# A two-layer decoder in fp32 on one core: the residual comes back in four pieces, and casts, remainders and token sums change places in their engines' orders

## What is computed

```python
def swiglu(h, w_gate_up, w_down):
    gu = h @ w_gate_up
    return (jax.nn.silu(gu[..., :D_FF]) * gu[..., D_FF:]) @ w_down

x = x + jnp.concatenate([main_out, mem_out], axis=-1) @ w_out[l]
return x + swiglu(rms_norm(x, ffn_norm[l]), w_gate_up[l], w_down[l])
```

## Time and profile before

| | |
|---|---|
| median of 3 runs | 3159.64 us |
| the profiled execution | 3156.6 us |
| its span in the trace | 3154.4 us |
| granted TensorE clock, mean over the span | 0.96 of full speed |
| PE busy | 2875.1 us (91% of the span) |
| DVE, ACT, POOL busy | 1487.3, 933.2, 1098.5 us |
| DMA queue | 257 MB, 25.4% of 16 engines |
| phase_ffn, layer 0 | from 1013.6 us to about 1704 us |
| phase_ffn, layer 1 | from 2448.3 us to about 3138 us |

### The profile page before, as it was taken

The page is one execution under the profiler, slowest core; times in us unless marked ns, Lnnn a source line. Parts: engine busy times, 40 slices in busy tenths (PEclk is TensorE's granted clock), DMA queues, the critical chain, the costliest instruction groups (busy, mean ns, idle before and its releaser), DMA issues. The chain is left out here.

```text
span 3154.4 us, 54822 instructions
## 1 busy us (share of the span) xinstructions
PE 2875.1 (91%) x23385; PEld 2311.3 (73%) x23385; DVE 1487.3 (47%) x2032; ACT 933.2 (30%) x1522; POOL 1098.5 (35%) x1050
## 2 busy tenths in 40 slices
PE   7999589888689999998999979969979999998998
PEld 5888367777557788886887767746648788886887
DVE  6233256666343655543223636547742755444222
ACT  3111334332143433332002123135542533332100
POOL 5343033333122444444334223311102344444332
PEclk9999699999799999999999989989989999999999
DMA  5332200000042232235223222233113133225321
GB/s 200 102 109 69 89 17 23 23 30 4 15 135 74 61 107 80 88 93 162 75 80 115 77 74 67 80 120 116 46 34 134 47 108 91 89 81 156 96 76 66
DMA packets 261081, 261.16 MB, mean 83 GB/s; under 512 B 9254, under 2 KB 221340, under 8 KB 259560
## 3 DMA queue, kind: packets, MB, share of 16 engines
q1 hardware_dynamic: 260088, 257.00, 25.4%
q10 hardware_dynamic: 272, 0.63, 0.1%
q0 software_dynamic: 480, 0.03, 0.0%
HBM read 186.80 MB, written 70.83 MB: 82 GB/s over the span
## 5 line engine op out<-in xcount | busy, mean ns | idle before, releaser
L276 POOL TENSOR_TENSOR w_lo_b<-w_raw_b,w_hi_b 128x512 fp32r<-128x512 f32 (+1 forms) x474 | 592.5, 1251 | 404.2 <-ACT w_hi_b L308 386.4
L358 PE MATMUL ps<-b_hi,w_hi_b 128*128 128x512 f32 x1176 | 459.2, 390 | 10.1 <-DVE b_lo L2233 7.3
L358 PE MATMUL ps<-b_lo,w_hi_b 128*128 128x512 f32 x1176 | 458.8, 390 | 0.0
L358 PE MATMUL ps<-b_hi,w_lo_b 128*128 128x512 f32 x1176 | 458.7, 390 | 0.0
L272 POOL CAST w_hi_b<-w_raw_b 128x384 fp32r<-128x384 f32 (+1 forms) x222 | 132.2, 596 | 799.5 <-PE ps L330 586.6
L358 PEld LDWEIGHTS ps<-b_hi,w_hi_b 128*128 128x128 f32 x1176 | 221.5, 188 | 57.8 <-DVE b_lo L2233 8.1
L330 PE MATMUL ps<-b_hi,w_hi_b 128*128 128x512 f32 x768 | 241.6, 396 | 22.2 <-DVE x_res L2308 22.2
L358 PEld LDWEIGHTS ps<-b_hi,w_lo_b 128*128 128x128 f32 x1176 | 221.5, 188 | 46.4
L358 PEld LDWEIGHTS ps<-b_lo,w_hi_b 128*128 128x128 f32 x1176 | 221.5, 188 | 45.8
L330 PE MATMUL ps<-b_lo,w_hi_b 128*128 128x512 f32 x768 | 239.9, 394 | 0.0
L330 PE MATMUL ps<-b_hi,w_lo_b 128*128 128x512 f32 x768 | 239.6, 393 | 0.0
(11 more groups left out here) (334 smaller groups left out, 5619.2 us busy)
## 6 DMA issues: line engine op xcount, KB each, us to landing
w_raw_b<-in_w_gate_up SPq DMA_DIRECT2D x88, 512.0 KB, 4.3
act_dram<-x_res SPq DMA_DIRECT2D x44, 512.0 KB, 6.0
stage<-act_dram SPq DMA_DIRECT2D x44, 512.0 KB, 3.6
w_raw_b<-in_w_down SPq DMA_DIRECT2D x32, 384.0 KB, 3.8
w_raw_a<-in_a_w_in SPq DMA_DIRECT2D x23, 512.0 KB, 4.7
u_dram<-evac_a SPq DMA_DIRECT2D x23, 512.0 KB, 3.0
w_raw_b<-in_w_down SPq DMA_DIRECT2D x32, 320.0 KB, 3.2
x_dram<-x_res SPq DMA_DIRECT2D x2, 4096.0 KB, 14.5
```

The lines of the kernel that those rows point to most:

```text
L276: nc.gpsimd.tensor_tensor(self.wlo[:, r, 0:n, :], source, self.whi[:, r, 0:n, :].bitcast(F32), ALU.subtract).then_inc(self.w_lo, 1)
L358: mm = self.nc.tensor.matmul(self.ps[:, bank, :], w[:, r, k, :], h[:, block, k, :], start=(start and k == 0 and a == 0 and h is self.bh), ...
```

## The change

It does seven things, all in `phase_ffn`:

1. The residual's H2 half comes back in four DMAs of 512 KB in place of two of 1 MB, in the order tiles 4-5, 0-1, 6-7, 2-3. The first stands right behind the store of feature tile 20 on SP, the second behind the load of tile 5, the third behind the store of feature tile 21, the fourth behind the load of tile 7.
2. `FF_ORDER` is 4, 5, 0, 1, 6, 7, 2, 3, and DVE waits for a piece ahead of each second addition of the first group.
3. In the last pair, DVE's remainders of tiles 2, 3 stand behind the addition to up, and those of tiles 4, 5 behind `scale_gate`.
4. The token sums stand in front of step k = 2 of the first projection.
5. On ACT `cast_sum(0)` and `cast_sum(1)` stand ahead of the first copy out of PSUM, and `cast_sum(2)` and the casts of weight blocks 2 to 4 have new places.
6. `silu(0)` stands behind the first copy of pair 1.
7. On DVE `sum_rest(0)` and `sum_rest(1)` stand ahead of `late_sums`.

The diff, cut to its core:

```diff
-FF_ORDER = [4, 5, 6, 7, 0, 1, 2, 3]
+FF_ORDER = [4, 5, 0, 1, 6, 7, 2, 3]
...
@@ SP
+                back = lambda tiles, semaphore: sp.dma_start(X[:, tiles, H2], self.x_dram[:, tiles, H2]).then_inc(semaphore, 16)
+                back(slice(4, 6), x_gate[0])
                 for t in range(2, groups[0][1]):
                     load_tile(t)
-                sp.wait_ge(act_full, FT)
-                sp.dma_start(X[:, HK:KT, H2], self.x_dram[:, HK:KT, H2]).then_inc(x_gate, 16)
+                sp.wait_ge(act_stored[0], 16 * (FT // 2))
+                back(slice(0, 2), x_up[0])
                 store(FT - 1)
-                for f in (FT - 2, FT - 1):
-                    sp.wait_ge(act_stored[f % 2], 16 * (f // 2 + 1))
-                sp.dma_start(X[:, 0:HK, H2], self.x_dram[:, 0:HK, H2]).then_inc(x_up, 16)
+                back(slice(6, 8), x_gate[1])
                 for g in range(G):
                     for i in range(KT):
                         load_upto(d0 + KT * g + i + 4)
                         if g + 1 < G and i < groups[g + 1][1]:
                             load_tile(groups[g + 1][0] + i)
+                        if g == 0 and i == 1:
+                            sp.wait_ge(act_stored[1], 16 * (FT // 2))
+                            back(slice(2, 4), x_up[1])
...
@@ ACT
-                for i in range(3):
+                for i in range(2):
                     self.cast_block(act, first(1) + i)
+                cast_sum(0)
+                cast_sum(1)
                 act.wait_ge(self.block_done, self.done(u0))
-                act.wait_ge(t_formed, 2)
                 copy(gate(0), ps[:, 0:2, :]).then_inc(snapped, 1)
-                for i in range(3, 5):
+                for i in range(2, 4):
                     self.cast_block(act, first(1) + i)
-                for n in range(3):
-                    cast_sum(n)
+                cast_sum(2)
+                self.cast_block(act, first(1) + 4)
...
                 cast_sum(3)
-                silu(0)
                 for f in range(1, FT):
...
                     copy(gate(f)[:, 0, :], ps[:, b, :]).then_inc(snapped, 1)
+                    if f == 1:
+                        silu(0)
...
@@ DVE
                 self.early_sums(dve, u0 + 2)
+                sum_rest(0)
+                sum_rest(1)
                 self.late_sums(dve, u0 + 2)
-                for n in range(3):
-                    sum_rest(n)
+                sum_rest(2)
...
-                    for t in range(4 if last else 0):
+                    for t in range(2 if last else 0):
                         tile_rest(t)
...
-                    for t in range(4, groups[0][1] if last else 4):
+                    for t in range(2, 4 if last else 2):
                         tile_rest(t)
...
                     scale_gate(f)
+                    for t in range(4, groups[0][1] if last else 4):
+                        tile_rest(t)
                     scale_up(f)
...
-                        if n == 0:
-                            dve.wait_ge(x_gate, 16)
-                        if n == HK:
-                            dve.wait_ge(x_up, 16)
+                        if n < KT and i % 2 == 0:
+                            dve.wait_ge((x_gate[0], x_up[0], x_gate[1], x_up[1])[i // 2], 16)
...
@@ PE
-                for t in range(TT):
-                    mm = mmul(ps[:, 6, t:t + 1], acc[:, t * P:(t + 1) * P], self.const("ones"), start=True, stop=True)
-                mm.then_inc(self.sums, 1)
-
...
+                def sum_tokens(k):
+                    if k == 2:
+                        for t in range(TT):
+                            mm = mmul(ps[:, 6, t:t + 1], acc[:, t * P:(t + 1) * P], self.const("ones"), start=True, stop=True)
+                        mm.then_inc(self.sums, 1)
+                    pe.wait_ge(self.h_lo, k + 1)
+
-                self.plain_gemm(pe, u0, base(0), operand, before_k=lambda k: pe.wait_ge(self.h_lo, k + 1))
+                self.plain_gemm(pe, u0, base(0), operand, before_k=sum_tokens)
```

2 lines of the change are left out of this document (1 added, 1 removed).

## The result

The changed kernel takes 3137.4 us (median of 4 runs, 3136.4 to 3140.3). The kernel before, run beside it on the same chip, takes 3158.1 us (median of 4). The ratio is 0.9939, with a 95% interval of 0.9921 to 0.9958: 20.6 us faster, where 22.4 were forecast, and 3137.2 us was the number. The profiled execution took 3140.3 us, its span is 3138.4 us, 16.0 less than before.

What follows compares the result with a forecast made beforehand. PE, busy for 91% of the span, was taken as the bound, with its pauses and the clock drops after them. 5.0 - 1.0 + 16.2 + 2.2 = 22.4 us off 3156.6 gives 3134.2, plus 3.0 makes 3137.2 us; range 3125 to 3148.

Steps and rivals of the forecast that it cites:

- start: Start of the phase through pair 1: one layer in each of two clock cases, gain 5.0 us in all.
- last pair: Last pair: the first piece ahead of tile 3's load delays it 0.5 us each layer, together -1.0.
- pause before strip 2: Before down strip 2: PE's pause falls from 10.96 to 2.9 us, gain 16.2 us over both layers.
- clock behind it: After the pause before strip 2: 1.7 us lost to half clock each layer, 5.6 together before; gain 2.2.
- the good case: Phase start: the clock rises at about 6 us in spite of the token sums; gain 4.5 us a layer.
- the bad case: Phase start: the token sums break the clock's rise, 14.4 us at half clock; gain 0.5 us a layer.
- Now the store goes at 1457.0: SP's queue before strip 2: last store at 1457.0, tile 6's cast starts at 1466.0, PE resumes at 1469.9.
- The bad clock case in both layers: Rival, phase start: the sums break the clock's rise in both layers; gain 18.4 us, 3141 us, chance 0.18.
- the good one in both layers: Rival, phase start: the sums do not matter to the clock in either layer; 26.4 us, 3133 us, chance 0.20.
- The crowding rival: Rival, before strip 2: four 512 KB transfers crowd, tile 6 some 3 us later, 6 us pause; 3143 us, chance 0.08.
- the change doesn't reach the pause: Rival, before strip 2: something unnamed holds tile 6 until the old moment; only 4 us gained, 3155.6 us, chance 0.04.
- a queue starts which makes PE wait in strip 0: Rival, tile loads: the piece ahead starts a queue, loads land after 14 us; slower, 3185 us, chance 0.02.

Runs made afterwards that it cites:

- sums_k1: The changed kernel with the token sums ahead of step k = 1 in place of k = 2; 3139.9 us (1 run).
- pieces_silu: The kernel before with only the four pieces, FF_ORDER, DVE's waits and silu(0) behind pair 1's first copy; 3137.3 us (5 runs), ratio 0.9935.
- piece2_late: The changed kernel with the second piece (tiles 0, 1) issued behind the last store and the third piece; 3139.3 us (1 run).
- sums_front: The changed kernel with the token sums back in front of the first projection; 3136.8 us (4 runs), ratio 0.9933.
- pieces_only: The kernel before with only the four pieces, FF_ORDER and DVE's waits for them; 3144.1 us (4 runs), ratio 0.9951.
- tiles_early_cast3: tiles_early with ACT's cast of tile 3 behind the copy of up in the last pair; 3120.9 us (4 runs), ratio 0.9873.
- tiles_early: The changed kernel with the loads of tiles 6 and 7 ahead of the last store, the second piece behind it; 3129.7 us (4 runs), ratio 0.9905.

## Why the prediction was right, and where it was not

| term, both layers | forecast | measured |
|---|---|---|
| start | 5.0 | 8.5 |
| last pair | -1.0 | -0.6 |
| pause before strip 2 | 16.2 | 13.45 |
| clock behind it | 2.2 | 1.1 |
| sum | 22.4 | 22.35 |

The first part of the table of phases holds the first two terms: 4.00 + 3.84 = 7.84, and with the 0.22 + 0.41 us that the last pair lost, the start gave 8.5.

**The start was mis-sized by 3.5 us, and the failed step is the choice between the two clock cases.** "I see them as equally likely in each layer and take one of each: 5.0 us in all" priced the good case at 4.5 a layer. It came in both layers (4.2 each). In all kernels with the sums two steps in or ahead the rise came at most 6.2 us after the projection's start. Only sums_k1, which puts the sums ahead of that point, brings out the bad case, and there it costs 1.6 us, not 4.0: the stretch at half clock grows by about the sums' own time. The text had the row that decides this. It had worked out 5.1 us to the sums and 6.2 us to the rise, so at most 1.1 us of the sums could stand ahead of it. And it had priced the bad case with 5.7 us more at half clock behind the sums, which no row had shown, and sums_k1 had 3.4 and 3.3. The working by parts was sound otherwise: silu's move alone gives 3.5 and 3.0 us, and the remaining 1 us comes with the casts and remainders (start part 455.7 / 455.6 in pieces_silu, 454.7 / 454.7 with them).

**The pause was mis-sized by 2.75 us, and the failed step is "Now the store goes at 1457.0".** The rest of the chain held: from the store's issue to the cast 8.64 us (forecast 9.0), from the cast to PE 4.05 (3.9). But the store was issued at 1462.33. This execution's phase began 7.75 us later and its start part was 4.00 shorter, so on the old time scale that is 1458.6, 1.6 us late. The reason is the sentence "Feature tile 21 ... comes about 1 us earlier". It came 0.6 us later (1462.31 on the old scale is 1458.6, against 1457.94). I had looked at what stands ahead of tile 21 on DVE, and not at what stands ahead of it on ACT, where silu and the up copy wait behind the cast of tile 5. Tile 5's load landed in 5.6 and 5.5 us. I had taken 3.5 from the earlier trace rows, a median. Two neighbours have come close to it, the load of tile 4 1.1 us ahead (2.8 before) and the second piece 0.4 us behind, and the table at piece2_late shows 0.9 us more with the first alone and 0.9 to 2 with both. The landings of stage's loads in the same stretch after, in the view of its DMAs, are longer as a whole, which doesn't say by what:

```profile
stage<-act_dram SPq DMA_DIRECT2D x10, 512.0 KB, 4.1
```

The median is 4.1 us, and was 3.5. How large the miss came out is in part this trace's own: with the same code the pause is 3.34 to 4.19 us in sums_front and sums_k1, so 0.4 to 1.3 us above the forecast's 2.9 in place of 1.4 and 1.5. The Trainium skill (DMA: Bandwidth & Descriptors, Rules for kernel authors) asks for 1 MiB or more per DMA for the most bandwidth. Taken alone, that speaks against the four pieces. The ratio of pieces_only, 0.9951, says that in this kernel the moment at which a transfer can start was worth more than its rate.

**The clock behind the pause.** 1.1 in place of 2.2 us: 5.5 and 2.9 us at half clock remained where 3.4 were taken for each, and the 5.2 us taken for layer 1 before were 4.8. A longer pause than forecast, 4.3 in place of 2.9, does not account for the difference between the layers, with 4.31 and 4.40 us.

**The last pair** lost 0.6, within the bounds 0 and 1.7 us a layer. The reason given, that the copy waits for the load of tile 3, is shown by tiles_early_cast3, and the landing grew from 4.1 and 4.0 us to 4.3 and 4.4. That the piece in front is what lengthened it is likely (4.1 to 4.7 us with it, 3.5 to 4.3 without), but the ranges overlap.

**The rivals.** The bad clock case in both layers (3141) is out, the good one in both layers (3133) is what happened in the start. The crowding rival (3143) had the 2.75 us in its direction, but not at its place: it had tile 6 land late behind the store, and from the store's issue to the cast took 8.64 us where 9.0 were forecast. Loads crowded each other one step earlier, at tile 5. That the change doesn't reach the pause, and that a queue starts which makes PE wait in strip 0, are both out: the chain is closed and strips 0 and 1 run without a pause. Of the prediction's own marks most came true: pair 1 below 1 us (0.98), the last pair 1.5 to 2.5 (1.70, 1.79), the rise at about 6 us or less. Two did not: the pause before strip 2 is 4.3 in place of near 3, and the load of tile 6 goes out 5.7 us earlier on the old scale (1464.54 is 1460.8, against 1466.45), not 8.

So the number was right because an excess of 3.5 us in the start covered shortfalls of 2.75 and 1.1 us at the pause and its clock, and that they cancel to 0.1 us is luck. The mechanisms were right but for the path by ACT's cast of tile 5, which was left out, and three sizes were off, in both directions.

## What to carry to other kernels

When a moved step's finish time is worked out, list what stands ahead of it on every engine it passes, not only on the one whose order was edited: here the last store hung on a transfer by way of ACT's cast of another tile. An engine that issues all DMAs in order makes every load wait for the slowest thing ahead of it, and moving two loads that were ready past one store that was not (tiles_early) was worth another 7.7 us (11.6 in the phases). Where several places are moved in one change, time the moves alone: of the seven here the four pieces with their order, and silu, carried nearly all of it. And before a pause's change in one trace is put down to an edit, look at that pause in other kernels with the same code there.

## What the runs showed of the hardware

- **One-column products and the clock.** 8 token sums in 16 matmuls of one column took 3.54 us at the lower clock and 1.84 us at the higher. Put into the stretch before the rise they moved it later by some 3.3 us, about their own time (sums_k1, one run, 9.5 and 9.4 us against at most 6.2). Ahead of the projection they brought it no sooner (5.3 and 5.1 us in sums_front, 2.8 to 6.2 in the others).
- **Pauses of equal length, with and without a drop.** Behind pauses of 1.70, 1.79, 1.83 and 1.92 us the clock stayed up, behind 1.80 (piece2_late) and 2.00 us (tiles_early) it was at 1.2 GHz for 3.4 us. Before strip 2 a pause of 4.31 us was followed by 5.5 us of it and one of 4.40 by 2.9. Between 1.8 and 4.4 us the length of the pause alone did not decide, so such a term had a spread of 1.3 to 1.7 us per pause in this kernel. The Trainium skill (TensorE: Matmul & The Clock Gate, What's actually happening) says that the same kernel runs a different number of its first matmuls at the lower clock from run to run. The spread of the rise, 2.8 to 6.2 us in kernels with the same start, agrees.
- **A load of 512 KB beside others.** The load of tile 5 landed in 3.4 and 3.7 us with the load ahead of it 2.8 us away, in 4.4 with it 1.1 us away (piece2_late), and in 4.4 to 5.6 with 512 KB more issued 0.4 us behind it as well. With the 512 KB behind it but the load ahead 2.5 us away it landed in 3.5 and 3.6 us (pieces_silu).
